# A third set of expert weight words, and the down product ahead of the up product, in a mixture-of-experts step on one Trainium2 core

## The chip, the core and the metric

The kernel runs on one NeuronCore of one Trainium2 chip. The core has a matrix engine (TensorE, PE in the profile; its weight loads are PEld), a vector engine (VectorE, DVE), a scalar engine (ScalarE, ACT), GpSimd (POOL) and SyncE (SP), which here only starts transfers. Each engine runs its own list of instructions and waits on semaphores. Sixteen DMA engines move data between HBM and the on-chip memory, which the kernel holds as one tensor `arena` of 128 partitions x 53200 float32 words. The metric is the device time of one execution in microseconds (us).

## The reference

One decoder block in float32 over 512 prompt tokens and 8 decode tokens (520 rows of width 1024): a mixing sublayer (a recurrent time mix, windowed attention with sinks, attention over a memory, gated and merged), then a sublayer of routed experts, each followed by a layer norm. What matters here is the second:

```
g_idx = argmax(x @ w_group + b_group);  g_w = its softmax value
top_v, top_i = top_k(router logits of that group, 2)        # 2 of 32 experts per row
gates = g_w * softmax(top_v)
for each expert e over its rows xb:                          # 32 experts, EXPERT_FF = 512
    h = silu(xb @ e_gate[e]) * (xb @ e_up[e]);  y = h @ e_down[e]
out = layer_norm(ALPHA * x + sum_k gates_k * y_k)
```

Each expert has three float32 matrices of 1024 x 512, 1024 x 512 and 512 x 1024, 2 MiB apiece. All 32 experts are computed, 192 MiB of weights in all.

## The kernel before

**Stages.** The mixing sublayer takes the first part of the program. After it PE makes the output projection and the router's logits (lines 1048 to 1069), VectorE turns the logits into an assignment (lines 1822 to 1953: the first and second best expert of each row, the rank of each row within its expert, and a table that says which row stands in which slot), and PE helps with two short groups of products (`rank_made`, `table_made`). Then the experts run one after another, each on one block of 64 slots; more than 64 rows of one expert would go to the extra blocks of `extra_blocks`. A closing stage reads the experts' outputs back, adds them to the rows and makes the last layer norm.

**One expert, e.** POOL gathers its rows from `X["x1"]` into `xg[e % 2]` by an indirect DMA (line 2077). PE turns them (`rows_step`, 4 transposes), ScalarE copies the result to `xgT`. PE makes the gate product (`gate_step`, 16 products of 64 x 256 accumulated in one bank) and the up product (`up_step`, the same size). ScalarE takes the sigmoid, VectorE multiplies sigmoid, gate and up into `hb` (`silu_step`, `h_step`). PE turns `hb` (`turn_h_step`, 2 transposes), VectorE copies it to `hT` (`hT_step`), PE makes the down product (`down_step`, 8 products of 64 x 512), VectorE copies the output to `yb` (`y_step`), and POOL scatters it to `X["ya"]` (line 2083).

**Order on PE.** It is written out by hand. `steady(e, ...)` interleaves expert e with the rest of expert e-1: gate product of e, turn of h of e-1, up product of e, turn of the rows of e+1, down product of e-1. A loop of 15 rounds of two steps covers experts 1 to 30, a last step without rows covers 31, and a turn and a down product close it.

**Weight words.** There are two sets: `eg[q]`, `eu[q]`, `ed[q]` with q = e % 2. SP starts all weight transfers in program order. The sets of experts 0 and 1 are started at lines 594 to 607, while the mixing sublayer ends. Then a loop (lines 619 to 627) starts, for e = 2 to 31, the gate weights of e when the gate product of e-2 is done, the up weights when its up product is done, and the down weights when its down product is done. The three counters `gate_mm`, `up_mm` and `y_mm` are raised by 2 ahead of the experts, so that "product of e-2 done" reads as a wait for e+1. SP is one list: while it waits for a product, what stands behind it waits too.

**Other engines.** VectorE and ScalarE run lists in step with PE: for each e, `silu_step(e)`, `hT_step(e-1)`, `h_step(e)`, the row indices for the gather of e+2, `y_step(e-1)`. The change leaves these lists as they are.

**Dead words.** From `R0` on (line 351, the words `ZSo` on, where the merged branch output lay) stand the routing variables: `LG`, `OH`, `earlier`, `SK`, `VB` and others. They are dead once the table is made. The words of `XTo` hold `x1T` until the logits are made, and later `xg`, `xgT`, `hb` and `hT`.

Of the kernel before, what the change touches and what calls it, by code (L numbers as in the profile page):

```python
# [20 lines left out]
P = 128  # L21
D = 1024
KD = D // P
T, B = 512, 8
N = T + B
# [18 lines left out]
SB = 64  # L44
# [99 lines left out]
h_made h_used x1_turned x1T_ready logits_made onehot_ready rank_made exp_asked exp_made  # L144
route_ready table_made table_ready
xg_in_a xg_in_b xg_turned xgT_ready gate_mm up_mm gate_act h_ready hT_turned hT_ready y_mm yb_ready
ew0g_in ew0u_in ew0d_in ew1g_in ew1u_in ew1d_in scat_a scat_b
# [8 lines left out]
def build(nc, I, O, X):  # L156

    with ExitStack() as ctx:
# [192 lines left out]
        R0 = [ZSo]  # L351
# [16 lines left out]
        OH = R(2, T5, NE)  # L368
        earlier = R(T5 + 1, NE)
# [7 lines left out]
        xe = R(XB, NE)  # L377
# [17 lines left out]
        yk = view(Fo, T5, 2, D)  # L395
        assert MGo + 2 * MGW >= Fo + 2 * EW and Fo + 3 * EW + 2 * D <= 53200
# [11 lines left out]
        hb, hT = M1(F2), M1(F2 // P, P)  # L408

# [19 lines left out]
        def _(sp):  # L429
# [177 lines left out]
            sp.dma_start(ed[1], wd[1]).then_inc(s["ew1d_in"], 16)  # L607

# [10 lines left out]
            with sp.Fori(0, NE // 2 - 1) as i:  # L619
                for q in range(2):  # L620
                    e = i * 2 + (q + 2)
                    sp.wait_ge(s["gate_mm"], e + 1)
                    sp.dma_start(eg[q], wg[bass.ds(e, 1)].rearrange("e p c n -> (e p) c n")).then_inc(s[f"ew{q}g_in"], 16)  # L623
                    sp.wait_ge(s["up_mm"], e + 1)
                    sp.dma_start(eu[q], wu[bass.ds(e, 1)].rearrange("e p c n -> (e p) c n")).then_inc(s[f"ew{q}u_in"], 16)
                    sp.wait_ge(s["y_mm"], e + 1)
                    sp.dma_start(ed[q], wd[bass.ds(e, 1)].rearrange("e p c n -> (e p) c n")).then_inc(s[f"ew{q}d_in"], 16)  # L627
# [16 lines left out]
        def _(pe):  # L644
# [426 lines left out]
            pe.wait_ge(s["onehot_ready"], 1)  # L1071
# [5 lines left out]
            pe.wait_ge(s["route_ready"], 1)  # L1077
# [4 lines left out]
            pe.wait_ge(s["table_ready"], 1)  # L1082
# [29 lines left out]
            def down(q):  # L1112
                for k in range(FF // P):
                    rows_of = hT[:, k % 2, (k // 2) * SB:(k // 2) * SB + SB]
                    for g in range(2):
                        last = mm(bank(5, D2)[g * SB:g * SB + SB, :], rows_of, ed[q][:, k, g * D2:g * D2 + D2],
                                  k == 0, k == FF // P - 1)
# [7 lines left out]
            def gate_step(e, q, n, first=False):  # L1125
# [3 lines left out]
                pe.wait_ge(s[f"ew{q}g_in"], n * 16 + 16)  # L1129
                gate(q)  # L1130
# [1048 lines left out]
```

## Time and profile before

| | us |
|---|---|
| median of 3 runs (1396.41 to 1400.54) | 1399.42 |
| the profiled execution, its own time | 1398.44 |
| its span in the profile | 1396.6 |
| busy: PE / PEld / DVE / ACT / POOL | 1146.1 / 796.6 / 436.1 / 238.7 / 109.9 |
| mean granted clock of TensorE | 0.926 of full speed (2.4 GHz) |
| read from and written to HBM | 274.97 MB and 24.23 MB |

Of the 32 transfers of each of the three kinds of expert weights, all 32 appear once, so no expert had more than 64 rows and the extra blocks did not run. The part of the span in which experts run goes from about 848 to 1344 us. The page cuts the span into 40 slices of 34.9 us; slices 26 to 38 lie within that part. In the timeline a row is one group of instructions of one line and engine: its start, its length, what it is, how many, and in brackets the idle time ahead of it with what ended it. All of PE's products have line 646 and all of its transposes line 651, since both go through a helper; each float32 product shows as two; a group of 32 with output 128x256 is one gate or one up product, 16 with 128x512 are one down product, 4 transposes are `rows_step` and 2 are `turn_h_step`. Neighbouring groups of the same line are merged, so a row of 64 or 48 products holds two of them. The rows of SPq are SP's starts of transfers, not the transfers.

### The profile page before, as it was taken

The page shows a single profiled execution, that of the slowest core. Times are in us where ns is not written, and L with a number is a line of the kernel's source. Part 1 is how long each engine was busy: PE and PEld are TensorE (multiplying, and loading weights), DVE is VectorE, ACT ScalarE, POOL GpSimd, SP SyncE. Part 2 cuts the span into 40 slices and gives each one's busy share as a digit, 9 for nine tenths or more (in the row PEclk, how much of TensorE's full clock was granted, in tenths as well). Part 3 has the DMA queues.
Part 4 walks back from the last instruction along what each step waited for, and adds up shares of the span by engine and source line. Part 5 has one row for each costly group of instructions (what it writes and reads, how often), then busy time and mean ns, then how long its engine had stood idle before and what let it go on. Part 6 is the DMA issues. An engine that isn't in the chain of part 4 may idle for free.

```text
span 1396.6 us, 21853 instructions
## 1 busy us (share of the span) xinstructions
PE 1146.1 (82%) x9283; PEld 796.6 (57%) x9283; DVE 436.1 (31%) x797; ACT 238.7 (17%) x400; POOL 109.9 (8%) x97
## 2 busy tenths in 40 slices
PE   4999989998989999998999836878787887878740
PEld 2788876777568878866864333434344443444320
DVE  5000003675446667433323271111111111111137
ACT  3100011244311121021111101111111111111001
POOL 3000000000000000000001101111111111111103
PEclk9999999999799999999999957999999999999975
DMA  7342242222130112153554034999999999999951
GB/s 276 121 150 75 75 138 72 71 68 68 31 77 25 48 30 54 46 198 114 201 198 176 31 152 136 390 426 425 426 416 424 414 425 418 414 420 420 420 201 61
DMA packets 47164, 290.78 MB, mean 208 GB/s; under 512 B 9204, under 2 KB 11318, under 8 KB 34027
## 3 DMA queue, kind: packets, MB, share of 16 engines
q1 hardware_dynamic: 41922, 281.41, 51.9%
q0 software_dynamic: 5184, 8.54, 1.8%
q8 instruction: 45, 0.74, 0.2%
q14 instruction: 13, 0.10, 0.0%
HBM read 274.97 MB, written 24.23 MB: 214 GB/s over the span
## 4 chain that ended last, share of the span: by engine, by line
PE 62%; DMA 25%; DVE 5%; issue 2%; ACT 2%; DVEq 1%; SPq 1%; POOL 0%; POOLq 0%; ACTq 0%
PE psum L646 59%; DMA arena<-in_e_up 17%; DMA arena<-in_e_gate 5%; PE psum L651 3%; DVE arena L1423 3%; DVE arena L1426 2%; ACT arena L1182 1%; DMA arena<-in_w_mem_kv 1%; DMA arena<-scratch_x,arena 1%; DMA arena<-in_p_abm 0%; SPq L627 0%; DVEq L2021 0%; POOL arena L2034 0%; SPq L623 0%; DVE arena L1441 0%
## 5 line engine op out<-in xcount | busy, mean ns | idle before, releaser
L646 PE MATMUL psum<-arena 64*64 64x64 f32 (+8 forms) x8760 | 1077.3, 341 | 155.5 <-DMA arena<-in_e_gate 60.6
L646 PEld LDWEIGHTS psum<-arena 64*64 64x64 f32 (+4 forms) x8760 | 738.1, 153 | 471.8 <-issue 214.2
L1182 ACT ACTIVATE arena<-psum 128x512 f32<-128x512 f32 (+8 forms) x151 | 94.6, 648 | 684.4 <-PE psum L646 397.1
L1423 DVE TENSOR_TENSOR arena<-arena,psum 128x256 f32<-128x256 f32 (+3 forms) x136 | 74.5, 548 | 403.5 <-PE psum L646 210.1
L1423 DVE TENSOR_TENSOR arena<-arena 128x1024 f32<-128x1024 f32 (+17 forms) x168 | 125.7, 758 | 195.8 <-PE psum L646 164.1
L651 PE MATMUL psum<-arena 128*128 128x128 f32 (+4 forms) x523 | 79.3, 288 | 42.6 <-DMA arena<-in_mem_prompt 13.3
L651 PEld LDWEIGHTS psum<-arena 128*128 128x128 f32 (+4 forms) x523 | 59.0, 151 | 74.8 <-issue 49.0
L2034 POOL TENSOR_TENSOR arena<-arena 128x1024 f32<-128x1024 f32 (+1 forms) x15 | 37.1, 2474 | 517.0 <-DVE arena L1423 517.0
L1423 DVE TENSOR_TENSOR arena<-psum,arena 128x256 f32<-128x256 f32 (+4 forms) x85 | 47.0, 564 | 66.8 <-PE psum L646 66.4
L2077 POOL DMA_INDIRECT arena<-scratch_x,arena x32 | 32.7, 1023 | 300.9 <-DVE arena L1972 300.3
L1401 ACT ACTIVATE arena<-psum 128x256 f32<-128x256 f32 x32 | 12.3, 383 | 247.7 <-PE psum L646 247.7
L1426 DVE SCALAR_TENSOR_TENSOR arena<-arena 128x520 f32<-128x520 f32 (+7 forms) x72 | 50.7, 716 | 11.5 <-DMA arena<-scratch_ya 7.1
L2083 POOL DMA_INDIRECT scratch_ya<-arena x32 | 32.5, 1015 | 138.6 <-DVE arena L1982 134.7
L1981 DVE COPY arena<-arena 128x1 uint32 (+1 forms) x32 | 4.9, 154 | 122.8 <-PE psum L646 122.8
L1401 ACT ACT_TABLE_LOAD x31 | 39.8, 1283 | 0.5
L1426 DVE SCALAR_TENSOR_TENSOR arena<-arena,psum 128x520 f32<-128x520 f32 (+2 forms) x9 | 9.1, 1013 | 64.9 <-PE psum L646 64.9
L1441 DVE BATCH_NORM_STATS2 arena<-arena 128x6 f32<-128x512 f32 (+1 forms) x30 | 19.3, 683 | 12.0 <-DMA arena<-in_x_prompt 11.2
L1982 DVE COPY arena<-psum 128x512 f32<-128x512 f32 x32 | 21.8, 680 | 0.0
L1270 ACT ACTIVATE arena<-arena 128x256 f32<-128x256 f32 x32 | 15.8, 495 | 33.5 <-DVE arena L1423 33.5
L1365 ACT ACTIVATE arena<-arena 128x1560 f32<-128x1560 f32 x8 | 12.0, 1503 | 49.1 <-DMA arena<-in_p_abm 49.1
L1426 DVE SCALAR_TENSOR_TENSOR arena<-psum,arena 128x2048 f32<-128x2048 f32 (+2 forms) x9 | 12.2, 1358 | 26.1 <-PE psum L646 26.0
L1199 ACT ACTIVATE arena<-arena 128x1024 f32<-128x1024 f32 (+1 forms) x15 | 18.6, 1240 | 8.3 <-DVE arena L1426 8.3
(105 smaller groups left out, 155.7 us busy)
## 6 DMA issues: line engine op xcount, KB each, us to landing
arena<-in_e_gate SPq DMA_DIRECT2D x32, 2048.0 KB, 16.8
arena<-in_e_up SPq DMA_DIRECT2D x32, 2048.0 KB, 21.9
arena<-in_e_down SPq DMA_DIRECT2D x32, 2048.0 KB, 12.6
arena<-in_w_in SPq DMA_DIRECT2D x46, 512.0 KB, 4.0
scratch_gates<-arena SPq DMA_DIRECT2D x24, 260.0 KB, 4.1
arena<-scratch_gates SPq DMA_DIRECT2D x8, 780.0 KB, 4.9
arena<-in_p_abm SPq DMA_DIRECT2D x8, 640.0 KB, 5.9
scratch_x<-arena SPq DMA_DIRECT2D x8, 512.0 KB
```

Of the source, the lines that this page charges most:

```text
L646: return pe.matmul(out, a, b, start=start, stop=stop)
L651: return pe.transpose(out, a, ident[b:b + n, b:b + n])
L1182: return act.activation(out, a, ACT.Copy)
L1199: act.activation(x[0:n, i, :], x[0:n, i, :], ACT.Identity, bias=nmr[0:n, i, :], scale=rstd[0:n, i, :]).then_inc(s["ln_scaled"], 1)
L1401: act.activation(esig, bank(2, F2), ACT.Sigmoid).then_inc(s["gate_act"], 1)
L1423: return v.tensor_tensor(out, a, b, op)
L1426: return v.scalar_tensor_tensor(out, a, sc, b, op0, op1)
L1441: v.bn_stats(st6[0:n, i, h, :], x[0:n, i, h * 512:(h + 1) * 512])
L1982: v.tensor_copy(yb[q], bank(5, D2)).then_inc(s["yb_ready"], 1)
L2034: g.tensor_tensor(x[0:n, i, :], x[0:n, i, :], gb[0:n, 1, :], ALU.add).then_inc(s["x_normed"], 1)
L2077: g.indirect_dma_start(xg[q], None, x1_halves, bass.IndirectOffsetOnAxis(ap=ix[:, q, :], axis=0), bounds_check=2 * N - 1, oob_is_err=False ...
L2083: g.indirect_dma_start(ya_halves, bass.IndirectOffsetOnAxis(ap=ix[:, 2 + q, :], axis=0), yb[q], None, bounds_check=4 * N - 1, oob_is_err=F ...
```

## The change

1. **A third set of weight words**, used once, for expert 2. Its gate and up words (`eg[2]`, `eu[2]`) lie behind the sigmoid's words and reach over the merged branch and the routing variables, which now start at `E2o + EW`. Its down words are four pieces `ed2[k]`: two in the dead part of `XTo`, one behind `eu[2]`, one behind `yb`. The variable `xe` moves onto words of `earlier`, `Osum` and `rank`, which are dead by then.
2. **SP** starts the gate weights of expert 2 right behind the down weights of expert 1, and its up weights and four down pieces when the gathers of experts 0 and 1 have landed. Experts 3 and 4 then take the sets of experts 0 and 1 as these come free; from 5 on each takes the set that the expert before last has left. The loop is shorter by two rounds.
3. **PE** makes in each step: gate product of e, turn of h of e-1, down product of e-1, up product of e, turn of the rows of e+1. Three steps stand ahead of the loop and two behind it.
4. The semaphores `onehot_ready`, `route_ready` and `table_ready` become three counts of one, `route_step`, and three new ones serve the third set.

```diff
-        R0 = [ZSo]
+        EW = KD * FF
+        E2o = Zo + 5120 + EW + F2
+        R0 = [E2o + EW]
...
         OH = R(2, T5, NE)
+        XE_AT = R0[0] - E2o - EW
...
-        xe = R(XB, NE)
+        xe = view(E2o + EW + XE_AT, XB, NE)
...
-        EW = KD * FF
-        eg = [view(Fo, KD, FF), view(Fo + EW, KD, FF)]
-        eu = [view(Zo + 5120, KD, FF), view(KKo, KD, FF)]
+        eg = [view(Fo, KD, FF), view(Fo + EW, KD, FF), view(E2o, KD, FF)]
+        eu = [view(Zo + 5120, KD, FF), view(KKo, KD, FF), view(E2o + EW, KD, FF)]
...
+        ed2 = [M1(D), M1(D), view(E2o + 2 * EW, D), view(Fo + 3 * EW + 2 * D2, D)]
...
             sp.dma_start(ed[1], wd[1]).then_inc(s["ew1d_in"], 16)
+            sp.dma_start(eg[2], wg[2]).then_inc(s["ew2g_in"], 16)
+            sp.wait_ge(s["xg_in_a"], 16)
+            sp.wait_ge(s["xg_in_b"], 16)
+            sp.dma_start(eu[2], wu[2]).then_inc(s["ew2u_in"], 16)
+            for k in range(FF // P):
+                sp.dma_start(ed2[k], wd[2][:, k, :]).then_inc(s["ew2d_in"], 16)
...
+            for q in range(2):
+                sp.wait_ge(s["gate_mm"], q + 3)
+                sp.dma_start(eg[q], wg[q + 3]).then_inc(s[f"ew{q}g_in"], 16)
+                sp.wait_ge(s["up_mm"], q + 3)
+                sp.dma_start(eu[q], wu[q + 3]).then_inc(s[f"ew{q}u_in"], 16)
+                sp.wait_ge(s["y_mm"], q + 3)
+                sp.dma_start(ed[q], wd[q + 3]).then_inc(s[f"ew{q}d_in"], 16)
+
+            def steady_load(e, q):
+                sp.wait_ge(s["gate_mm"], e + 1)
+                sp.dma_start(eg[q], one(wg, e)).then_inc(s[f"ew{q}g_in"], 16)
...
-            with sp.Fori(0, NE // 2 - 1) as i:
+            with sp.Fori(0, NE // 2 - 3) as i:
                 for q in range(2):
...
+                    steady_load(i * 2 + (q + 5), q)
+            steady_load(NE - 1, 0)
...
-            def steady(e, q, n, before, after):
-
-                gate_step(e, q, n)
-                turn_h_step(*before)
-                up_step(e, q, n)
-                if after:
-                    rows_step(*after)
-                down_step(*before)
+            def steady(e, q, n, gq, gn, down_q, down_n, last=False):
+                gate_step(e, gq, gn)
+                turn_h_step(e - 1)
+                down_step(e - 1, down_q, down_n)
+                up_step(gq, gn)
+                if not last:
+                    rows_step(e + 1, 1 - q, n + q)
...
-            with pe.Fori(0, NE // 2 - 1) as i:
-                e = i * 2
-                steady(e + 1, 1, i, (e, 0, i), (e + 2, 0, i + 1))
-                steady(e + 2, 0, i + 1, (e + 1, 1, i), (e + 3, 1, i + 1))
+            steady(1, 1, 0, 1, 0, 0, 0)
+            steady(2, 0, 1, 2, 0, 1, 0)
+            steady(3, 1, 1, 0, 1, 2, 0)
+            with pe.Fori(0, NE // 2 - 3) as i:
+                steady(i * 2 + 4, 0, i + 2, 1, i + 1, 0, i + 1)
+                steady(i * 2 + 5, 1, i + 2, 0, i + 2, 1, i + 1)
             last_n = NE // 2 - 1
```

PE's list of the step of expert 1 before (`64x256` is a gate or up product, `64x512` a down product, `128x128` a transpose; `ew1g_in` is the arrival of the gate weights in set 1):

```order
490 L646 MATMUL psum<-arena 64x256 [waits ew1g_in]
491 L646 MATMUL psum<-arena 64x256 x15
492 L651 MATMUL psum<-arena 128x128 [waits h_ready]
493 L651 MATMUL psum<-arena 128x128
494 L646 MATMUL psum<-arena 64x256 [waits ew1u_in]
495 L646 MATMUL psum<-arena 64x256 x15
496 L1122 ISA
497 L651 MATMUL psum<-arena 128x128 [waits xg_in_a]
498 L651 MATMUL psum<-arena 128x128 x3
499 L646 MATMUL psum<-arena 64x512 [waits yb_ready,ew0d_in,hT_ready]
500 L646 MATMUL psum<-arena 64x512 x7
```

The same step, and the first product of the next, with the change:

```order
486 L670 MATMUL psum<-arena 64x256 [waits ew1g_in,h_ready,xgT_ready]
487 L670 MATMUL psum<-arena 64x256 x15
488 L675 MATMUL psum<-arena 128x128 [waits h_ready]
489 L675 MATMUL psum<-arena 128x128
490 L670 MATMUL psum<-arena 64x512 [waits yb_ready,ew0d_in,hT_ready]
491 L670 MATMUL psum<-arena 64x512 x7
492 L670 MATMUL psum<-arena 64x256 [waits ew1u_in]
493 L670 MATMUL psum<-arena 64x256 x15
494 L675 MATMUL psum<-arena 128x128 [waits xg_in_a]
495 L675 MATMUL psum<-arena 128x128 x3
496 L670 MATMUL psum<-arena 64x256 [waits ew2g_in,h_ready,xgT_ready]
```

The down product moved from behind the rows' transposes to right behind the transposes of h, and the next gate product now follows the rows' transposes directly. (A float32 product is one instruction here and two in the profile, so 16 here are 32 there; a transpose is one in both.)

SP's list from the weights of expert 1 on, before:

```order
160 L606 DMA arena<-in_e_up 128x4096 [waits h_made]
161 L607 DMA arena<-in_e_down 128x4096
162 L619 UNCONDITIONAL_BRANCH
163 L619 ISA
164 L623 ISA [waits gate_mm]
165 L623 DMA arena<-in_e_gate 128x4096
166 L625 DMA arena<-in_e_up 128x4096 [waits up_mm]
167 L627 DMA arena<-in_e_down 128x4096 [waits y_mm]
```

and with the change:

```order
160 L610 DMA arena<-in_e_up 128x4096 [waits h_made]
161 L611 DMA arena<-in_e_down 128x4096
162 L612 DMA arena<-in_e_gate 128x4096
163 L615 DMA arena<-in_e_up 128x4096 [waits xg_in_b,xg_in_a]
164 L617 DMA arena<-in_e_down 128x1024 x4
165 L634 DMA arena<-in_e_gate 128x4096 [waits gate_mm]
166 L636 DMA arena<-in_e_up 128x4096 [waits up_mm]
167 L638 DMA arena<-in_e_down 128x4096 [waits y_mm]
```

Six starts of transfers (2048 KB, 2048 KB and four of 512 KB) now stand ahead of the first wait for a product, and that wait is for expert 0's product on behalf of expert 3.

## Rows read from the trace of the kernel before

**Rows 1.** The span in 40 slices: DMA share in tenths, GB/s.
```profile
DMA  7342242222130112153554034999999999999951
GB/s 276 121 150 75 75 138 72 71 68 68 31 77 25 48 30 54 46 198 114 201 198 176 31 152 136 390 426 425 426 416 424 414 425 418 414 420 420 420 201 61
```
**Rows 2.** PE's waits from 840 to 1345: releaser, us, times, longest.
```profile
PE psum L646 <- DMA arena<-in_e_gate: 60.6, 29, 2.9
PE psum L646 <- DMA arena<-in_e_up: 28.5, 20, 1.8
```
**Rows 3.** Stretches: length, busy per engine with counts, PEclk, DMA share, GB/s.
```profile
815.00:830.00 15.00, 1.70 (x6) 1.57 (x6) 11.99 (x52) 0.21 (x1) 0.00 (x0) 0.50 0.11 46
850.00:855.00 5.00, 4.55 (x22) 2.65 (x24) 0.00 (x0) 1.68 (x2) 0.00 (x0) 0.50 0.00 0
871.00:872.00 1.00, 1.00 (x6) 0.28 (x4) 0.00 (x0) 0.98 (x2) 0.96 (x1) 1.00 0.00 0
900.00:1000.00 100.00, 79.40 (x548) 41.39 (x546) 12.70 (x38) 15.03 (x20) 14.29 (x14) 0.97 1.01 426
```
**Rows 4.** Timeline of SP: starts of the weights of experts 1 and 2.
```profile
803.96 0.43 SPq L607 DMA_DIRECT2D arena<-in_e_down  x1
857.30 0.34 SPq L623 DMA_DIRECT2D arena<-in_e_gate  x1
860.60 0.34 SPq L625 DMA_DIRECT2D arena<-in_e_up  x1
874.48 0.33 SPq L627 DMA_DIRECT2D arena<-in_e_down  x1
```
**Rows 5.** Timeline of PE: experts 0 and 1.
```profile
848.59 1.12 PE L651 MATMUL psum<-arena 128*128 128x128 f32 x4 [11.16 <-DMA arena<-scratch_x,arena]
850.45 10.10 PE L646 MATMUL psum<-arena 128*64 128x256 f32 x64 [0.75 <-ACT arena L1182]
860.49 0.66 PE L651 MATMUL psum<-arena 128*128 128x128 f32 x4
862.01 3.68 PE L646 MATMUL psum<-arena 128*64 128x256 f32 x32 [0.86 <-ACT arena L1182]
865.62 0.44 PE L651 MATMUL psum<-arena 128*128 128x128 f32 x2
865.99 3.68 PE L646 MATMUL psum<-arena 128*64 128x256 f32 x32
870.78 7.11 PE L646 MATMUL psum<-arena 128*64 128x512 f32 x48
```
**Rows 6.** Timeline of DVE: silu and copy of hT in the step of expert 1.
```profile
866.14 0.42 DVE L1423 TENSOR_TENSOR arena<-arena,psum 128x256 f32<-128x256 f32 x1 [5.05 <-ACT arena L1401]
866.48 0.42 DVE L1976 COPY arena<-psum 128x256 f32<-128x256 f32 x1
```
**Rows 7.** Timeline of PE: gate product of 3, down product of 2, gate product of 6.
```profile
887.74 3.68 PE L646 MATMUL psum<-arena 128*64 128x256 f32 x32 [1.70 <-DMA arena<-in_e_gate]
...
899.46 3.66 PE L646 MATMUL psum<-arena 128*64 128x512 f32 x16
...
951.44 5.36 PE L646 MATMUL psum<-arena 128*64 128x256 f32 x32 [2.40 <-DMA arena<-in_e_gate]
```
**Rows 8.** Timeline of PE and DVE: expert 31, the end of the experts.
```profile
1326.54 5.36 PE L646 MATMUL psum<-arena 128*64 128x256 f32 x32 [2.16 <-DMA arena<-in_e_gate]
...
1340.50 3.66 PE L646 MATMUL psum<-arena 128*64 128x512 f32 x16 [0.81 <-DVE arena L1976]
...
1335.93 0.42 DVE L1423 TENSOR_TENSOR arena<-arena,psum 128x256 f32<-128x256 f32 x1 [2.82 <-PE psum L646]
...
1339.44 0.68 DVE L1982 COPY arena<-psum 128x512 f32<-128x512 f32 x1
```
**Rows 9.** DMA issues of the page: size, median us to landing.
```profile
arena<-in_w_in SPq DMA_DIRECT2D x46, 512.0 KB, 4.0
arena<-scratch_x,arena POOLq DMA_INDIRECT x32, 8.1
```

More of the change, by code:

```diff
@@ L408, in build @@
         hb, hT = M1(F2), M1(F2 // P, P)
+        ed2 = [M1(D), M1(D), view(E2o + 2 * EW, D), view(Fo + 3 * EW + 2 * D2, D)]
+        assert E2o + 2 * EW + D <= ZSo + SF * N and Fo + 3 * EW + 2 * D2 + D <= 53200
         block = ctx.enter_context(nc.Block())
@@ L1115, in down @@
                     for g in range(2):
-                        last = mm(bank(5, D2)[g * SB:g * SB + SB, :], rows_of, ed[q][:, k, g * D2:g * D2 + D2],
+                        last = mm(bank(5, D2)[g * SB:g * SB + SB, :], rows_of, (ed2[k] if q == 2 else ed[q][:, k, :])[:, g * D2:g * D2 + D2],
                                   k == 0, k == FF // P - 1)
@@ L1123, in rows_step, with gate_step @@
                 turn_rows(q)
-            def gate_step(e, q, n, first=False):
+            def gate_step(e, gq, gn, first=False):
                 pe.wait_ge(s["xgT_ready"], e + 1)
@@ L1128, in gate_step, with up_step, turn_h_step @@
                     pe.wait_ge(s["h_ready"], e)
-                pe.wait_ge(s[f"ew{q}g_in"], n * 16 + 16)
-                gate(q)
-            def up_step(e, q, n):
-                pe.wait_ge(s[f"ew{q}u_in"], n * 16 + 16)
-                up(q)
-            def turn_h_step(e, q, n):
+                pe.wait_ge(s[f"ew{gq}g_in"], gn * 16 + 16)
+                gate(gq)
+            def up_step(gq, gn):
+                pe.wait_ge(s[f"ew{gq}u_in"], gn * 16 + 16)
+                up(gq)
+            def turn_h_step(e):
                 pe.wait_ge(s["h_ready"], e + 1)
@@ L1141, in down_step @@
                 pe.wait_ge(s["hT_ready"], e + 1)
-                pe.wait_ge(s[f"ew{q}d_in"], n * 16 + 16)
+                pe.wait_ge(s[f"ew{q}d_in"], n * 16 + 16 if q < 2 else 16 * (FF // P))
                 pe.wait_ge(s["yb_ready"], e + 1)
                 down(q)
-            def steady(e, q, n, before, after):
-                gate_step(e, q, n)
-                turn_h_step(*before)
-                up_step(e, q, n)
-                if after:
-                    rows_step(*after)
-                down_step(*before)
+            def steady(e, q, n, gq, gn, down_q, down_n, last=False):
[5 more added lines that the diff above has]
+                    rows_step(e + 1, 1 - q, n + q)
             rows_step(0, 0, 0)
             gate_step(0, 0, 0, first=True)
-            up_step(0, 0, 0)
+            up_step(0, 0)
             rows_step(1, 1, 0)
-            with pe.Fori(0, NE // 2 - 1) as i:
-                e = i * 2
-                steady(e + 1, 1, i, (e, 0, i), (e + 2, 0, i + 1))
-                steady(e + 2, 0, i + 1, (e + 1, 1, i), (e + 3, 1, i + 1))
+            steady(1, 1, 0, 1, 0, 0, 0)
[4 more added lines that the diff above has]
+                steady(i * 2 + 5, 1, i + 2, 0, i + 2, 1, i + 1)
             last_n = NE // 2 - 1
-            steady(NE - 1, 1, last_n, (NE - 2, 0, last_n), None)
-            turn_h_step(NE - 1, 1, last_n)
-            down_step(NE - 1, 1, last_n)
+            steady(NE - 2, 0, last_n, 1, last_n - 1, 0, last_n - 1)
+            steady(NE - 1, 1, last_n, 0, last_n, 1, last_n - 1, last=True)
+            turn_h_step(NE - 1)
+            down_step(NE - 1, 0, last_n)
             def extra(i):
@@ L1870, in _ @@
                 last = tt(earlier[:, t + 1, :], earlier[:, t, :], Osum[:, t, :], ALU.add)
-            last.then_inc(s["onehot_ready"], 1)
+            last.then_inc(s["route_step"], 1)
             v.wait_ge(s["exp_made"], 1)
```

38 lines of the change are left out of this document (19 added, 19 removed).

## The prediction

> **What bounds the kernel now.** I read the slices of the page first, then PE's waits, then the timelines of SP and PE at the two ends of the experts' stage.
>
> In the slices [rows 1] the reader is to see that from slice 26 to 37 the DMA engines are at 9 tenths and 414 to 426 GB/s, and that slice 23 stands at 3 tenths and 31 GB/s, so there is idle transfer time just ahead of a stage that is full of transfers. In PE's waits [rows 2] it is to see that all through the stage PE waits for weights: 60.6 us in 29 waits for gate weights and 28.5 us in 20 for up weights, none for down weights. The gate products of experts 3 and 31 start when their weights arrive, at 887.74 and 1326.54 [rows 7, 8]. That is (1326.54 - 887.74) / 28 = 15.67 us per expert, or 5.22 us per 2 MiB load with its share of gathers and scatters. PE's own step is 3.61 us for gate, 0.37 for the turn, 3.61 for up, 0.6 for the rows, 3.61 for down (starts to starts of [rows 5]), 11.8 us. So the stream of weights bounds the stage. What counts is when this stream becomes gapless, how many loads are left then, and what PE has to do after the last gate weights arrive.
>
> Before, the stream has two gaps. After the weights of expert 1 (last start at 803.96) nothing is loaded until 857.30, when the gate product of 0 is done [rows 4]; the share is 0.11 in 815 to 830 and 0.00 in 850 to 855 [rows 3]. The two loads started at 857.30 and 860.60 are over by about 869.5, and the third waits for the down product of 0, which stands last in PE's step of expert 1, until 874.48 [rows 4]; at 871 to 872 the share is 0.00 [rows 3]. From 874.48 on it is gapless.
>
> **The change part by part.**
>
> *Third set.* The gate weights of 2 go out at about 804.5 and take 5.2 us of the idle stretch before 830. The up and down weights of 2 wait for both gathers. PE starts on the first at 848.59 [rows 5]; the second was started 1.4 us later, so SP goes on at about 850.3 and the stream runs from about 851.3, 7 us earlier than before and with one load less. If the stream stayed full from there, it would gain 7 + 5.2 + the gap of about 5.5 = 18 us. It will not: the third set is used only once, and from expert 5 on SP again waits for PE to leave a set. I follow PE.
>
> *PE's new step.* Two latencies that were covered now stand open. The down product follows the turn of h at once, and needs hT. VectorE's copy ran 866.48 to 866.90, behind the silu that ScalarE's sigmoid releases [rows 6], while the turn ended at 865.99 [rows 5]. So the down product starts at about 866.95, a stall of 0.96 us. The gate product follows the turned rows at once and needs xgT. That distance is visible where rows and gate already stand side by side: 860.49 to 862.01, 1.52 us for both, of which 0.86 is the wait [rows 5]. New step at full clock: 3.61 + 0.37 + 0.96 + 3.61 + 3.61 + 1.52 = 13.68 us, 1.9 more than before, and still under 15.67.
>
> *Where the stream is filled.* PE reaches the gate product of 1 at 862.01 as before [rows 5]. Steps 1 to 4 have their weights in time (the stream from 851.3 brings up and down of 2 by 864, gate and up of 3 by 874), so PE sets the pace: the gate product of 4 starts at 862.01 + 3 x 13.68 = 903.05, the down product of 3 starts 3.61 + 0.37 + 0.96 later and ends 3.66 after that, at 911.7. This is what SP waits for to start the down weights of 5, behind which the gate weights of 6 are free to go. By then the queue has run dry in three places: gate of 5 waits for the gate product of 3 (893.0), up of 5 for its up product (901.5), down of 5 until 911.7. From 911.7 on there is no further gap: down weights are asked for 8 us after the gate weights of the same parity arrive, with two loads still queued.
>
> The same event stands in the trace before: a down load started into an empty queue at 874.48, the gate weights behind it arriving at 887.74, 13.26 us later [rows 4, 7]. So the gate weights of 6 arrive at 911.7 + 13.26 = 925.0. PE is ready for them only at 930.4, gains 2 us per step and is waiting for weights again from expert 9. The gate weights of 31 then arrive at 925.0 + 25 x 15.67 = 1316.7, against 1326.54: **-9.8 us**. This one event carries the sum; a later start of the stream at 851.3, by up to about 8 us, would not move it.
>
> The four pieces of 512 KB have no price in it. A load of 512 KB lands 4.0 us after its start [rows 9], the four are started back to back, and even 6 us more would only fill the gaps before 911.7. The Trainium skill ("DMA: Bandwidth & Descriptors", Bandwidth, Where 436 GB/s comes from) says that for HBM to SBUF transfers an HBM limit of about 358 GB/s binds. The trace shows 426 GB/s over 100 us with all engines on weights [rows 3], so it disagrees. By the page's figure a load would take 6.1 us, the queue would not run dry before 912, the same stretch of backlog would have delayed the kernel before by 8 us more, and the gain would come out near 16 us, an estimate from that page; the measured rate is what I use.
>
> *The end.* Before, from the arrival of the gate weights of 31 to the start of the last down product PE takes 1340.50 - 1326.54, and 3.66 more, 17.6 us [rows 8]. After: gate product 5.3 (as long as there), turn 0.37, stall 0.96, down of 30 3.61, up of 31 3.61. Then h is no longer covered by a down product: the up product ended at about 1335.8 and VectorE had h at 1336.35 [rows 8], 0.6; the copy of y (0.83 with its index) now sits between h and the copy of hT (0.4), so the last down product starts about 1.85 us after the up product and ends 5.5 after it. Sum 19.4: **+1.8 us**. If that gate product runs at full clock (3.68), the end costs +0.1.
>
> *Nothing else.* The semaphores that become one count the same three events in the same order. The moved `xe` and the routing words change no length. In the steady part the earlier y frees the down set 5 us sooner, but the queue was never empty there, so this is worth nothing; both new stalls and the single longer wait lie under the 15.67 us.
>
> **Sum.** -9.8 + 1.8 = -8.0 us with the last gate product at 5.36 us as in the profile, -9.7 with it at 3.68. In the profile 10 of 31 gate products take 5.36 us instead of 3.68 (one of them in [rows 7]), so I take -8.9. Against the profiled execution's own time, 1398.44 - 8.9 = 1389.5; against the median 1399.42, which is 1.0 higher, 1390.5. I forecast 1390.5 us. Its own range: every 1 us on PE's path from 862 to 911.7 moves the end by 1 us. Taking the stall of 0.96 between 0.5 and 1.5 makes +-2 us over the four steps, one 5.36 us product there +1.7. That gives 1387 to 1394.
>
> **The rivals.**
>
> *The whole cover, -16 us, 1383.* The stream stays full from 851.3. For it speaks that ten loads of 5.22 us would end at 903.5. Against it that the down product of 3 would have to be done by then, 8 us earlier than PE can be, unless its steps took 11.6 us.
>
> *The gathers come late, about -4 us, 1395.* The row indices of e+2 are made after the up product of e, which moved to the end of the step. A gather takes 8.1 us to land [rows 9], with about 1.8 us to start it: 10 us of the 13.7 to the next rows' turn while PE sets the pace. If landing takes 13 us under the fuller queue, each of three steps loses 1 to 2 us. In the trace before PE waits for a gather only once in the stage after the first.
>
> *The clock turns the stream's slack into a bound; slower.* Place: every step from 9 on. PE needs 13.68 us at full clock and has 15.67, so it becomes the bound from 1.2 half-clock products per step on (5.36 instead of 3.68, 1.7 us each). With two of these per step it needs 17.0, 1.4 more than the stream, over 22 steps +31 us, less the 8: about 1422. For it speaks that waits of 2.2 to 2.4 us came ahead of 5.36 us products [rows 7, 8], and that the two waits of a step become one of about 2 us. Against it that after waits of the same length most products took 3.68 us, 12 took 5.36 in 31 steps before, and never two in a step. The Trainium skill ("TensorE: Matmul & The Clock Gate", Loop structure matters more than you think) says that a loop that waits for DMA ahead of each product lets the clock fall. By that rule each step would have one 5.36 us product, 15.4 us, still under 15.67: the sum would be -8.0. The trace agrees only in part, since 1.70 us of waiting ahead of the gate product of 3 left it at 3.68 [rows 7].
>
> *The new order gives back what the third set gains; no change.* It would need 2 us more on each of four steps than I count, with the last gate product at 5.36: a stall at every hT of 3 us instead of 1.
>
> **How the numbers follow.** Forecast case 0.75; whole cover 0.04; late gathers 0.12; given back 0.05; clock bound 0.04. A difference of 0.3% (4 us) is about what a measurement of this kernel can tell from none: the bound is 1395.2. Faster: the forecast case, the whole cover and half of the late gathers, 0.85; the same: the other half and the given-back case, 0.11; slower 0.04. For the range I start from 1387 to 1394, and widen it by the runs' own spread of 2 us each way and toward the late gathers: 1384.5 to 1396.
>
> **What would show it.** Right: a load of gate weights at about 804.5 and six starts at about 850 in SP's timeline; a DMA share near 0 in spots between 893 and 912 and full after that; rows and gate 1.5 us apart, turn and down 1.3 us; gate products at 15.67 us distance from expert 9 or 10 on; the gate product of 31 near 1316.7 and the last down product over near 1335 to 1336. Wrong: the gate product of 4 far from 903; gaps in the stream after 915; waits of PE for gathers after the first; a step without a wait for weights late in the stage.

## The result, and the profile after

| | kernel before | changed kernel |
|---|---|---|
| first comparison, median us | 1397.91 (4 runs, 1396.06 to 1400.54) | 1382.34 (4 runs, 1380.81 to 1388.80) |
| second comparison, median us | 1396.21 (17 runs) | 1383.81 (5 runs, 1382.23 to 1386.06) |
| ratio, first and second | | 0.9899 (0.9866 to 0.9931), 0.9911 (0.9898 to 0.9924) |
| profiled execution: time, span | 1398.44, 1396.6 | 1388.80, 1387.0 |

The change makes the kernel 12.4 us faster by the sharper of the two ratios (10.6 to 14.2). I forecast 1390.5 us, about 9 under the median then known, with a range from 1384.5 to 1396. The direction held. Both measured medians, 1382.34 and 1383.81, lie below the range. (A fifth run of the changed kernel in the first comparison took 1385.42 us. It is in the ratio, and not in the median of four.)

A quantity that does not hang on the rest of the kernel is the length of the experts' stage, from the first row transposes of expert 0 to the end of the last down product. In the two profiles this is 495.6 us before (848.59 to 1344.16) and 483.6 after (851.09 to 1334.67). The part ahead of it was 2.5 us longer in the profile after; a later profile of the same kernel reached it at 846.64, so this is spread.

The slices after, against [rows 1]: the slice from about 798 to 832 us carries 213 GB/s instead of 152, and the one from 902 to 936 reads 333 where the stream still has gaps.

```profile
DMA  7342231312121101252646055989999999999941
GB/s 278 121 151 76 76 132 65 85 46 70 52 67 37 48 25 44 61 172 70 232 152 266 31 213 177 400 333 425 427 425 424 427 424 426 420 412 426 422 185 61
```

PE's waits after, from 840 to 1345, against [rows 2] (us in total, times, longest):

```profile
PE psum L670 <- DMA arena<-in_e_gate: 48.6, 22, 3.3
PE psum L670 <- DVE arena L2002: 28.4, 32, 0.9
PE psum L670 <- ACT arena L1208: 7.8, 10, 1.0
```

The waits for up weights are gone, those for gate weights are 22 instead of 29 (48.6 us instead of 60.6), and the two stalls of the new order are there: 32 times 0.9 us for hT (line 2002), and 0.69 to 0.97 for xgT (line 1208).

SP's starts after, against [rows 4]:

```profile
806.69 0.76 SPq L612 DMA_DIRECT2D arena<-in_e_gate  x1
851.50 0.33 SPq L615 DMA_DIRECT2D arena<-in_e_up  x1
...
894.85 0.34 SPq L642 DMA_DIRECT2D arena<-in_e_gate  x1
903.09 0.34 SPq L644 DMA_DIRECT2D arena<-in_e_up  x1
913.24 0.33 SPq L646 DMA_DIRECT2D arena<-in_e_down  x1
```

The last three are the gate, up and down weights of 5. The stretches around them, against [rows 3] (length, busy per engine, clock, DMA share, GB/s):

```profile
890.00:900.00 10.00, 8.41 (x59) 4.06 (x59) 1.65 (x6) 2.27 (x3) 2.06 (x2) 1.00 0.99 395
900.00:905.00 5.00, 4.03 (x38) 2.48 (x34) 1.19 (x4) 1.31 (x2) 0.54 (x1) 1.00 0.59 193
905.00:910.00 5.00, 4.10 (x36) 2.31 (x33) 0.76 (x2) 0.95 (x2) 1.51 (x2) 1.00 0.93 368
910.00:915.00 5.00, 5.00 (x36) 2.29 (x34) 0.00 (x0) 0.00 (x0) 0.00 (x0) 1.00 0.43 112
```

The queue runs dry ahead of the second and of the third of these starts, as the prediction laid it out. The third dry place that it named, ahead of the gate weights of 5, is hardly there: the worst microsecond around that start, 895 to 896, still carries 303 GB/s. Against 426 GB/s the four stretches lack 7.8 us of transfer.

PE after, at the start of the stage (against [rows 5]), the gate product of 4, and the end (against [rows 8]):

```profile
851.09 1.12 PE L675 MATMUL psum<-arena 128*128 128x128 f32 x4 [11.40 <-DMA arena<-scratch_x,arena]
...
864.29 3.68 PE L670 MATMUL psum<-arena 128*64 128x256 f32 x32 [0.69 <-ACT arena L1208]
867.90 0.44 PE L675 MATMUL psum<-arena 128*128 128x128 f32 x2
869.25 7.12 PE L670 MATMUL psum<-arena 128*64 128x512 f32 x48 [0.90 <-DVE arena L2002]
...
904.60 3.68 PE L670 MATMUL psum<-arena 128*64 128x256 f32 x32 [0.97 <-ACT arena L1208]
...
1317.43 3.68 PE L670 MATMUL psum<-arena 128*64 128x256 f32 x32 [1.07 <-DMA arena<-in_e_gate]
1321.04 0.44 PE L675 MATMUL psum<-arena 128*128 128x128 f32 x2
1322.38 7.12 PE L670 MATMUL psum<-arena 128*64 128x512 f32 x48 [0.90 <-DVE arena L2002]
1330.02 0.44 PE L675 MATMUL psum<-arena 128*128 128x128 f32 x2 [0.52 <-DVE arena L1449]
1331.01 3.66 PE L670 MATMUL psum<-arena 128*64 128x512 f32 x16 [0.55 <-DVE arena L2002]
```

A row of 48 products holds the down product and the up product. The three steps from 864.29 to 904.60 took 40.31 us, 13.44 each.

### The profile page after: what moved, and what is told of

Read it like the earlier page. It is cut to its first block, busy times and chain, and to the rows that moved or that the text cites. A ratio compares the mean times of both kernels' runs of the same rounds, so it can differ in the third digit from the quotient of the medians.

```text
span 1387.0 us, 21834 instructions
## 1 busy us (share of the span) xinstructions
PE 1144.7 (83%) x9283; PEld 799.9 (58%) x9283; DVE 434.3 (31%) x797; ACT 239.0 (17%) x400; POOL 110.0 (8%) x97
## 4 chain that ended last, share of the span: by engine, by line
PE 65%; DMA 20%; DVE 6%; issue 3%; ACT 3%; DVEq 2%; SPq 1%; POOL 0%; POOLq 0%; ACTq 0%
PE psum L670 63%; DMA arena<-in_e_gate 18%; DVE arena L1449 3%; PE psum L675 3%; ACT arena L1208 2%; DVE arena L1452 2%; DMA arena<-in_w_mem_kv 1%; DVEq L1992 1%; ACT arena L1427 1%; DMA arena<-scratch_x,arena 0%; DMA arena<-in_p_abm 0%; DVEq L2047 0%; POOL arena L2060 0%; DVE arena L1467 0%; SPq L646 0%
## 5 line engine op out<-in xcount | busy, mean ns | idle before, releaser
L670 PE MATMUL psum<-arena 64*64 64x64 f32 (+8 forms) x8760 | 1073.2, 341 | 146.7 <-DMA arena<-in_e_gate 48.6
L1220 ACT ACTIVATE arena<-arena 128x1 f32<-128x1 f32 (+1 forms) x15 | 4.4, 295 | 77.8 <-DVE arena L1469 77.7
```

Of the source, the lines that this page charges most:

```text
L670: return pe.matmul(out, a, b, start=start, stop=stop)
```

## The experiments

Theory A is the prediction's: PE's pace up to the down product of 3 fixes when the stream of weights is full for good, and the bytes left then, at their rate, and PE's work after the last gate weights make the rest. Three rivals were put against it: that the change gains outside the stage (B), that the early down product itself carries the gain (C), and that the early start of the stream does (the rival of experiment 5). All kernels ran beside the kernel before, and the ratio is to it. The last column is left empty where PE no longer waits for the last gate weights, so that their arrival does not show.

| kernel | ratio (95%) | stage us | last gate weights, from the stage's start |
|---|---|---|---|
| before, first profile / again | 0.9998 (0.9981 to 1.0015) | 495.6 / 493.5 | 477.95 / 475.85 |
| changed, first profile / again | 0.9911 (0.9898 to 0.9924) | 483.6 / 482.0 | 466.34 / 464.77 |
| third set, old order | 0.9895 (0.9880 to 0.9911) | 480.2 | 463.19 |
| new order alone | 0.9981 (0.9969 to 0.9993) | 492.5 | 473.57 |
| changed, later start | 0.9922 (0.9899 to 0.9946) | 482.6 | 465.36 |
| three sets in turn | 0.9889 (0.9875 to 0.9904) | 479.2 | 460.28 |
| the same, old order | 0.9898 (0.9879 to 0.9918) | 480.0 | 462.43 |
| the same, down pieces early | 0.9908 (0.9889 to 0.9928) | 482.1 | 464.42 |
| changed, loads in matching order | 0.9866 (0.9844 to 0.9888) | 475.2 | - |
| three sets, matching order | 0.9868 (0.9848 to 0.9888) | 473.9 | - |
| the same, down pieces early | 0.9843 (0.9819 to 0.9867) | 470.9 | - |

**1. The changed kernel again.** No edit.

> The changed kernel unaltered. In its first profile the experts' stage (first transposes of rows of expert 0 to the end of the last down product) took 851.09 to 1334.67, 483.6 us, against 495.6 before, while the part ahead of it was 2.5 us longer. Theory A (the stage alone gains, the part ahead of it only varies): stage again 482 to 486 us, median 11 to 13 us under the kernel before. Theory B (the change gains outside the stage too, which the first profile missed): start of the stage earlier than 848, median 15 us or more under.

Stage 482.0 us, start of the stage at 846.64, the median 12.4 us under the kernel before. A holds, B does not: its bound of 848 was passed, but the kernel before reached its stage at 845.23 in its own second profile, and the 12.4 us (10.6 to 14.2) agree with the 11.5 to 12.0 by which like stages differ (experiment 2). The gain lies in the stage.

**2. The kernel before again.** No edit.

> The kernel before, unaltered, for the spread of one profile: its experts' stage was 495.6 us with 13.4 us from the first transposes to the gate product of 1 and 17.6 us after the last gate weights, against 13.2 and 12.6 us and twice 17.2 in two profiles of the changed kernel. If these differences belong to the change, the same 495 to 496 us again; if they are spread, 493 to 496.

Stage 493.5: spread. Its first gate and up products took 8.66 us instead of 10.10 [rows 5], because the clock rose earlier: the granted clock was 1.00 from 851 us on, 5.8 us after the start of the stage, and in the first profile only from 857 on, 8.4 us after it. The end after the last gate weights took again 17.62:

```profile
845.23 1.12 PE L651 MATMUL psum<-arena 128*128 128x128 f32 x4 [11.51 <-DMA arena<-scratch_x,arena]
847.09 8.66 PE L646 MATMUL psum<-arena 128*64 128x256 f32 x64 [0.75 <-ACT arena L1182]
...
1321.08 5.36 PE L646 MATMUL psum<-arena 128*64 128x256 f32 x32 [2.16 <-DMA arena<-in_e_gate]
```

So profiles with about the same length of this first group are to be compared: 495.6 to 483.6 (10.10 and 10.06 us) and 493.5 to 482.0 (8.66 and 8.75). The stage gains 12.0 and 11.5 us.

**3. The third set with the old order of PE's step.**

```diff
                 gate_step(e, gq, gn)
                 turn_h_step(e - 1)
-                down_step(e - 1, down_q, down_n)
                 up_step(gq, gn)
                 if not last:
                     rows_step(e + 1, 1 - q, n + q)
+                down_step(e - 1, down_q, down_n)
```

> The third set of weight words stays, PE's step is put back to gate, turn of h, up, rows, down. Theory A (PE's pace up to the down product of 3 fixes the stream, and the new order opens two stalls): the down product of 3 ends about 1.6 us sooner after the start of the stage than in the changed kernel, the end after the last gate weights takes 16 to 17.6 instead of 17.2, the stage 480 to 482 us, median 1 to 4 us under the changed kernel. Theory C (the early down product is what frees the weight words, and carries part of the gain): the stage 487 us or more.

Stage 480.2, and not slower than the changed kernel (the intervals of the ratios overlap; the trace has it 1.9 to 3.4 us shorter). The down weights of 5 start 59.2 us after the start of the stage (849.83) against 62.15 and 60.74. C falls: with the third set in place the new order gains nothing. By the one trace with the like first group (8.72 us against 8.75) it costs 1.9 us; the ratios do not tell the two apart (medians 1382.65 and 1383.81).

```profile
909.01 0.33 SPq L646 DMA_DIRECT2D arena<-in_e_down  x1
```

**4. The new order alone.** In the kernel before, `down_step` is moved in `steady` to stand ahead of `up_step`.

> Two sets of weight words as before, only the new order of PE's step. Theory A: the down weights of 2 start 3.6 us sooner after the start of the stage than before (26.0 to about 22.2 us), the gate weights of 31 come 3.9 us sooner, the end costs 0 to 1.8 more: 2 to 4 us under the kernel before. Theory C: 5 us or more under. The opposite, stalls that cost: 0 or slower.

The down weights of 2 start 21.1 us after the start of the stage (849.96) instead of 25.9 and 24.6 in the two profiles before, the last gate weights come 4.4 and 2.3 us sooner than in them, and the end takes 18.9. Stage 492.5, ratio 0.9981, 2.7 us (1.0 to 4.3): A's 2 to 4. The two halves of the change do not add: 2.7 us alone, nothing or less beside the third set.

```profile
871.06 0.33 SPq L627 DMA_DIRECT2D arena<-in_e_down  x1
```

**5. The stream starts later.**

```diff
             sp.wait_ge(s["xg_in_b"], 16)
+            sp.wait_ge(s["gate_mm"], 3)
             sp.dma_start(eu[2], wu[2]).then_inc(s["ew2u_in"], 16)
```

> The changed kernel, with the start of the up and down weights of 2 held back until the gate product of 0 is done, 6.6 to 7.3 us later. Theory A (what counts is the down product of 3, since the stream would run dry there anyway): stage 482 to 484, no difference to the changed kernel beyond 1 us. Rival (the early start of the stream is what gains): 6 to 7 us slower than the changed kernel.

The up weights of 2 start at 7.5 us of the stage instead of 0.5, the down weights of 5 at 61.0:

```profile
854.22 0.33 SPq L616 DMA_DIRECT2D arena<-in_e_up  x1
...
907.70 0.33 SPq L647 DMA_DIRECT2D arena<-in_e_down  x1
```

Stage 482.6 against 482.0 in the profile with the like start, ratio 0.9922 (0.9899 to 0.9946) against 0.9911. Seven us of transfer time taken away cost nothing that these figures can tell, and the rival's 6 to 7 us are excluded. This is the sharpest test of the step on which the sum was built, and it holds.

**6. Three sets in turn.** Expert e in set e mod 3, and PE's loop of six steps; SP:

```diff
-            def steady_load(e, q):
-                sp.wait_ge(s["gate_mm"], e + 1)
+            def ring_load(e, q):
+                sp.wait_ge(s["gate_mm"], e)
...
-            with sp.Fori(0, NE // 2 - 3) as i:
-                for q in range(2):
-                    steady_load(i * 2 + (q + 5), q)
+            with sp.Fori(0, 9) as i:
+                for q in range(3):
+                    ring_load(i * 3 + (q + 3), q)
...
```

> As the changed kernel, but the three sets are used in turn (expert e in set e mod 3) instead of the third once; PE's list is a loop of six steps. Theory A (the stream runs dry between the gate product of 3 and the down product of 3 because a set has to come free): no gaps after 852, all loads 5.2 us apart, the gate weights of 31 arrive about 456 us after the start of the stage instead of 466, the stage 473 to 475 us, median 9 to 11 us under the changed kernel. Rival (PE's pace or the stream's rate is the bound already): stage 482 to 486 as in the changed kernel.

Half a miss. The gaps are gone (423 GB/s from 890 to 900, 418 from 900 to 910), but the last gate weights arrive at 460.3 and not 456, the stage takes 479.2, not 473 to 475, and the ratio puts it 3 us under the changed kernel, not 9 to 11 (0.9889 against 0.9911, and the intervals just overlap).

```profile
1300.00:1307.73 7.73, 5.10 (x42) 3.35 (x39) 1.14 (x4) 0.60 (x1) 1.00 (x1) 1.00 0.81 345
1307.73:1325.00 17.27, 15.29 (x94) 7.72 (x96) 2.17 (x6) 1.67 (x2) 0.99 (x1) 0.90 0.24 99
```

These rows say how: the rate falls to 345 GB/s ahead of the arrival of the last gate weights at 1307.73, and 99 GB/s x 17.27 us = 1.7 MB move after it, where two loads of 2.1 MB are still due. So at least 2.5 MB of loads that stand behind the gate weights had already moved when these were complete (some of what moves later is rows that POOL gathers and scatters). In the kernel before 193 x 13.46 = 2.6 MB were left:

```profile
1326.54:1340.00 13.46, 13.15 (x84) 7.40 (x84) 1.81 (x5) 1.67 (x2) 0.64 (x1) 0.87 0.47 193
```

My reading is that the 16 engines do not finish a load together, that with more loads queued the first of them run further ahead, and that a load lands with the last of them. That is an inference from the bytes and is not shown; no row has the engines apart. The count of loads from the start of the stream, by which I came to 456, leaves this out. The prediction's own sum for a stream that stays full does not: 18 us sooner than the 477.95 of the first profile before is 460.0, since the arrival it starts from was late by the same effect. In addition the last gate product took 5.33 us here and 3.68 in the changed kernel.

**7 and 8. Three sets in turn, the old order; and three down pieces of expert 2 loaded early.**

```diff
+            sp.wait_ge(s["logits_made"], 1)
+            for k in (0, 1, 3):
+                sp.dma_start(ed2[k], wd[2][:, k, :]).then_inc(s["ew2d_in"], 16)
             sp.wait_ge(s["xg_in_a"], 16)
             sp.wait_ge(s["xg_in_b"], 16)
             sp.dma_start(eu[2], wu[2]).then_inc(s["ew2u_in"], 16)
-            for k in range(FF // P):
-                sp.dma_start(ed2[k], wd[2][:, k, :]).then_inc(s["ew2d_in"], 16)
+            sp.dma_start(ed2[2], wd[2][:, 2, :]).then_inc(s["ew2d_in"], 16)
```

> Three sets in turn and PE's old order. Theory A: the stream is gapless in both orders, so the last gate weights arrive 460 us after the start of the stage as with the three sets in the new order, and the end is shorter by 0.3 to 1.9 us: stage 476.5 to 479, 0 to 2 us under the three sets in the new order.

> As the one before, and three of the four down pieces of expert 2 (1.5 MiB) are loaded when the logits are made, in the stretch in which no weights move. Theory A (the stage now lasts as long as its bytes take, 5.25 us per 2 MiB): 3.9 us less stream, stage 473 to 475. Rival (PE's pace bounds by now): no difference.

Both miss, by 1 and by 7 us, and the early pieces gain nothing (of the 2.1 us by which their stage is longer, 1.5 lie in the first gate and up products, 10.13 us against 8.67). The stretches show the same gap in both, first the old order, then with the early pieces:

```profile
870.00:880.00 10.00, 10.00 (x78) 5.34 (x76) 1.51 (x4) 1.93 (x3) 2.00 (x2) 1.00 0.81 290
```

```profile
860.00:870.00 10.00, 9.48 (x76) 5.35 (x74) 1.24 (x4) 2.56 (x4) 1.45 (x2) 1.00 0.68 288
870.00:880.00 10.00, 10.00 (x82) 5.61 (x80) 1.99 (x6) 0.68 (x2) 1.03 (x1) 1.00 0.79 281
```

SP stood at the down weights of 3, whose words come free at 25 us of the stage in the old order, while the gate weights of 4, whose words were free at 16, stood behind them. I had followed the bytes and forgotten the list. It is the step that I had got right for the down weights of 5.

**9 to 11. The loads in the order in which words come free.** PE's new order leaves and needs gate words of e, down words of e-1, up words of e. SP's list follows it (here with two sets, from expert 7 on; the first six experts written out in the same manner):

```diff
-            def steady_load(e, q):
-                sp.wait_ge(s["gate_mm"], e + 1)
...
-                sp.wait_ge(s["up_mm"], e + 1)
...
-                sp.wait_ge(s["y_mm"], e + 1)
...
+            def in_turn(e, q):
+                gate_in(e, q, e + 1)
+                down_in(e - 1, 1 - q, e)
+                up_in(e, q, e + 1)
```

> The changed kernel, the third set used once as there, but SP's list in the order in which PE's new step leaves and needs the words: gate weights of e, down weights of e-1, up weights of e, instead of gate, up, down of e. Theory A, carried on: the gate weights of 6 no longer stand behind the down weights of 5, which wait for the down product of 3, so one load more fits into the gaps (up to 5 us), and the last gate weights are followed by three loads instead of two, so that the end hangs on one load after the down product of 30 (2.8 us): stage 474 to 477 instead of 482 to 483.6, median 6 to 8 us under the changed kernel. Rival (the order of the loads is of no account, since their sum is what bounds): stage 482 or more.

> Three sets in turn, PE's new order, and SP's list in the matching order. Theory A: no gap at all, 89 loads of 5.22 us from 1.5 us after the start of the stage, and 6 to 8 us after the last of them: stage 473 to 476, against 479.2 with three sets in turn and the loads as gate, up, down.

> As the one before, and three of the four down pieces of 2 are loaded when the logits are made. Theory A: 3.9 us of loads less in the stage, of which the wait for the gate product of 0 gives back about 1.6: stage 471 to 473.5. In the order gate, up, down this piece gained nothing, since the down weights of 3 then waited for the down product of 0 with an empty queue.

All three land in or at A's ranges: 475.2, 473.9 and 470.9 us. Ratios 0.9866, 0.9868 and 0.9843. The first needs nothing but SP's list, its interval (0.9844 to 0.9888) lies clear of the changed kernel's, and its rows show both effects that were foreseen:

```profile
900.00:905.00 5.00, 4.12 (x37) 2.55 (x36) 1.15 (x4) 1.88 (x2) 2.06 (x2) 1.00 0.89 298
905.00:910.00 5.00, 4.10 (x22) 1.53 (x22) 0.76 (x2) 0.38 (x1) 0.00 (x0) 1.00 0.97 376
...
1305.66 3.68 PE L684 MATMUL psum<-arena 128*64 128x256 f32 x32 [0.74 <-ACT arena L1222]
1309.27 0.44 PE L689 MATMUL psum<-arena 128*128 128x128 f32 x2
1310.60 3.66 PE L684 MATMUL psum<-arena 128*64 128x512 f32 x16 [0.90 <-DVE arena L2016]
1315.68 3.68 PE L684 MATMUL psum<-arena 128*64 128x256 f32 x32 [1.42 <-DMA arena<-in_e_up]
```

The gaps are smaller. Between 885 and 925 us, where all of them lie, the list in matching order moves 381 GB/s and the changed kernel 353, in the profiles with the like first group (8.72 and 8.75 us). Against the 424 GB/s of the long stretch from 930 to 1290 that is 2.6 us of transfer gained, an estimate from these rates; the rest of the 6.8 us is left for the end. There PE waits for the up weights and not for the gate weights: the down product of 30 is over before the last but one load arrives. With this list the third set in turn adds little to its single use (473.9 against 475.2, the ratios alike). The early pieces, worth nothing in experiment 8, bring 3.0 us of stage here (473.9 to 470.9; the ratios' intervals overlap). Experiment 8 differs in PE's order too, so it is not shown that the list alone makes this difference. Nor was PE's old order tried with a list of its own (gate of e, up of e, down of e-1), so what the new order of PE is worth together with the matching list is open. With three sets, the matching list and the early pieces the kernel is 21.9 us faster than before (0.9843), 0.7% under the changed one, and the best here.

## Why the prediction was wrong

The mechanism held: the stream has to wait for the down product of 3, and what is left after that sets the time. What failed is sizes. Within the stage the gain was 12.0 us and not 8.9, and the largest error was the step called the end, put at +0.9 us and measured at -0.4. But 12 us alone would have stayed inside the range. What took the result out of it was the level: the sum started from 1399.42 us, a median of three runs, and the range allowed 2 us for such spread, where about 5 were needed. Point by point, by the prediction's own steps:

- **The bound and the gaps: right.** The stream of weights bounds the stage, two gaps stood in it, and the third set does not fill it since it is used once. The late start (7 us later without a loss that shows) and the gaps at two of the three places that were forecast show it. One reading of [rows 1] is wrong: the slice with 3 tenths carries 152 GB/s, and the 31 GB/s belong to the slice ahead of it. Nothing in the sum hangs on it.
- **PE's pace: right in kind, 0.9 us too slow.** The stalls were taken as 0.96 and 0.86; they are 0.90 and mostly 0.69. A step takes 13.44 instead of 13.68, and the down weights of 5 start 62.15 us after the start of the stage instead of 63.1 (60.74 in the second profile, where the clock rose 1.3 us earlier, which the kernel before has as well).
- **The rate: 0.8 us.** From that start to the last gate weights the forecast had 13.26 + 25 x 15.67 = 405.0 us. It took 404.2 and 404.0. The kernel before has this spread by itself: from the start of the down weights of 2 to the last gate weights it took 452.1 us in the first profile, from which I took the rate, and 451.3 in the second. So this part is no error of the mechanism, and in the second pair most of it falls away.
- **The end: the term that was mis-sized most.** Forecast +1.8 or +0.1, +0.9 in the sum. Measured 17.24 us twice against 17.62 twice: -0.4. The way from the up product to the last down product is 1.4 us and not 1.85, because VectorE's copy of y is over 0.4 us before I had it, and the last gate product took 3.68 us in each profile of the changed kernel. At 5.35 (new order alone) the end was 18.9, so the choice between the two lengths of that product, which I counted half, is real, and worth 1.7 us.
- **Sum.** Stage -8.9 forecast. In the like pairs -12.0 and -11.5; for the first of them 0.9 of the difference from the pace, 0.8 from the rate, 1.3 from the end. All three erred to one side.
- **The range: the step that put the forecast outside.** The right size, -12 from 1399.42, would have given 1387.4, inside the range. The measured medians are 5.1 and 3.6 us lower. This is the level: the kernel before stood at 1397.9, 1396.2, 1395.1 and 1394.9 us in the four comparisons, under the median of three runs that I started from. In the first comparison 1.5 us come from that; the other 3.6 are the scatter of four runs, which spread over 8 us (by medians the gain is 15.6 us there and 12.4 in the second comparison). I widened the range by 2 us for this, and it took 4 to 5.
- **The rivals.** PE became the bound for single steps only: twice in the changed kernel's profile a gate product took over 6.5 us, the step then took 16.4 and 16.5 us, more than 15.67, and the next gate weights were there before PE was. The mean rate from 930 to 1290 us was 424 GB/s all the same, and the arrival of the last gate weights shows no mark of it. The gathers were never waited for after the first. The whole cover did not come from this kernel, but it did come from three sets in turn: the stream carries 416 GB/s from 850 to 925 us, and the stage of 479.2 us and the ratio of 0.9889 (15.5 us) meet that rival's -16 us, which from 495.6 is 479.6. Three sets with the matching list and the early pieces go 8.7 us below it.

```profile
1098.74 6.59 PE L670 MATMUL psum<-arena 128*64 128x256 f32 x32 [3.12 <-DMA arena<-in_e_gate]
...
1115.17 3.68 PE L670 MATMUL psum<-arena 128*64 128x256 f32 x32 [0.87 <-ACT arena L1208]
...
1271.14 5.36 PE L670 MATMUL psum<-arena 128*64 128x256 f32 x32 [2.69 <-DMA arena<-in_e_gate]
...
1286.62 3.68 PE L670 MATMUL psum<-arena 128*64 128x256 f32 x32 [1.14 <-DMA arena<-in_e_gate]
...
1302.03 5.36 PE L670 MATMUL psum<-arena 128*64 128x256 f32 x32 [2.77 <-DMA arena<-in_e_gate]
```

- **The weighed rules.** The trace after the change has 426 GB/s over 70 us (930 to 1000), so it too disagrees with the sentence of the Trainium skill by which about 358 GB/s bind ("DMA: Bandwidth & Descriptors", Bandwidth, Where 436 GB/s comes from). I read that section too narrowly: it sets a measured 425 GB/s for 16 MB beside this figure, and with that the trace agrees. The rule on a long DMA wait between products ("TensorE: Matmul & The Clock Gate", Loop structure matters more than you think) holds for 10 of the 22 gate products of the changed kernel's profile that waited for their weights. These ten took 5.0 to 6.7 us, all behind waits of 2.69 to 3.23 us. Two behind waits of 2.62 and 3.25 us took 3.68, and so did all ten behind waits of 1.78 us or less.

The rows above also suggest why the slow products come mostly in every other step: a product that takes 1.7 us longer makes PE later, so the next wait is shorter by about as much (2.69, 1.14, 2.77, and 1.07 ahead of the last), and behind the short wait the product is fast again. That is read from one profile and argued, not shown; no run tested it. The wait alone does not decide: in the kernel before, gate products of 5.3 us stand behind waits of 2.16 to 2.55 us, and one of 3.68 behind 2.88. Open is what else does, and whether the last product of the changed kernel always takes 3.68 us; the three profiles with this order and this set say so (the third is experiment 5), which is few.

## What to carry to other kernels

When one engine issues all loads in one list, write the list in the order in which the consumer leaves the words, and check it against the order in which it needs them. A buffer more is worth only what the list lets through: here a third set in turn brought about 3 us beyond its single use (their intervals overlap), and the reordered list 6 to 7 with no further memory. To price a prefetch, find the last load that waits for the consumer with an empty queue: a gain ahead of it is lost there unless it also makes the consumer earlier, and what comes later is bytes over rate. And start a range from the spread between comparisons, not from three runs of one.

## What the runs showed of the hardware

- When the last gate weights were complete, two loads of 2.1 MB, 4.2 MB in all, stood behind them, and less than that was left to move: 2.6 MB in the kernel before, 140 GB/s x 14.57 us = 2.0 MB in the changed one, and 1.7 MB with three sets in turn (all bytes, POOL's rows among them). What was left falls with the time by which the last load, the down weights of 31, had been started ahead of that moment: 2.1 us before, 5.1 us in the changed kernel, 20.7 us with three sets in turn. The two halves of the change fit in: 1.6 us and 2.8 MB with the third set and the old order, 6.8 us and 1.8 MB with the new order alone. So loads that were started later do move bytes before an earlier one is complete. That this delays the load that is waited for is my reading; experiment 6 is the case for it.

```profile
1324.43 0.33 SPq L627 DMA_DIRECT2D arena<-in_e_down  x1
```

```profile
1312.36 0.33 SPq L646 DMA_DIRECT2D arena<-in_e_down  x1
```

- The stream of three sets with the matching list and early pieces does not end sharply: it runs at 415 GB/s in 1290 to 1300, 329 in 1300 to 1305 and 221 in 1305 to 1310.

```profile
1290.00:1300.00 10.00, 7.62 (x56) 3.69 (x54) 1.14 (x4) 0.60 (x1) 0.00 (x0) 1.00 0.98 415
1300.00:1305.00 5.00, 4.10 (x36) 2.30 (x34) 0.75 (x2) 1.26 (x2) 1.01 (x1) 1.00 0.78 329
1305.00:1310.00 5.00, 3.68 (x22) 1.21 (x20) 0.00 (x0) 0.41 (x1) 0.00 (x0) 1.00 0.52 221
```

- Four transfers of 512 KB (4 KB per partition) in a full queue cost no rate against one of 2 MiB (16 KB per partition). With three sets in turn every third expert's down weights come as four pieces, a ninth of the bytes, and the stream carries 424 GB/s from 930 to 1290 us, as in the changed kernel without such pieces.
